# Retention values of a hybrid decoder layer by seven block products, with strided residue units between them

## The chip, the cores and the metric

One core of a Trainium2 chip runs the kernel. The metric is the device time of one execution in microseconds. Before the change it was 1881.49 us, the median of three runs (1881.42 to 1882.46). The work lies on these engines: PE (TensorE, matmuls; PEld its weight loads), DVE (VectorE), ACT (ScalarE), POOL (GpSimd, here also the accumulating DMAs) and SP (SyncE, which issues most DMAs).

## What is computed

Two decoder layers over 512 tokens of width 1024. Each projects the normed input once and mixes tokens in two ways in parallel. Cut to what matters here:

```python
def hybrid_layer(x, g_mix, w_in, ...):
    hn = rmsnorm(x, g_mix)
    proj = hn @ w_in
    qa, ka, va, qr, kr, vr, gr, ga, gb = split(proj)
    # A: dilated attention, 3 head groups with dilations 1, 4, 16 (va: 3 x 512 columns)
    # B: retention, 4 heads of 256 value columns (vr: 1024 columns)
    ...
    x = x + (sigmoid(ga) * y_a + sigmoid(gb) * y_b) @ w_o
    x = x + square(relu(rmsnorm(x) @ w_up)) @ w_down
```

The change is in how `va` (for the dilated groups) and `vr` are made, the value stage at the head of each layer.

## The kernel before

The program writes one instruction list for each engine by hand; engines meet through semaphores only. So the order in each list is the order of work. A layer consists of a value stage, four pairs of heads (queries, keys, attention, retention), gates, the output projection and the MLP. Weights are in single precision. To multiply them, ScalarE rounds each unit of weights (128 x 2048) to `w_hi` in two halves (`hi_halves`, L704 on), VectorE subtracts for `w_lo` (`lo_half`, L1175 on), and TensorE multiplies three terms (hi x hi, hi x lo, lo x hi). There are two buffers of `w_hi` and `w_lo`, and one of raw weights, `raw`, which SyncE fills half by half as VectorE is done with it (`lo_done`). The same split is made of the normed input: `h_hi`, `h_lo`, eight tiles of 128 x 512 (channels by tokens), counted by `h_ready`.

The value stage (`values_half`, L1925) has five groups g of 512 value columns, each of two units: g 0 for the attention group of dilation 1, g 1 and 2 for the retention's values, g 3 and 4 for the two attention groups that are ordered by residue (token modulo 4). A group has four banks of PSUM for the four token blocks and takes 96 matmuls of 512 columns. The banks of g 0 and g 1 differ (`vbanks`), and a group waits (`v_out`) for the evictions of the one two before it. For g 3 and 4, ScalarE copies `h_hi` and `h_lo` in residue order into `res_hi` and `res_lo` (`by_residues`, L745). The evictions scale with the token's inverse RMS. Retention values are split into hi and lo there (`vR_high`, L804, and VectorE's L1301), sent to DRAM by `vR_away` (L546), and brought back head by head by `vR_back` as `vR_hi`, `vR_lo` and `vR_last`.

After group 0, TensorE makes the mean of squares (`mean`), ScalarE its root (`rms`, L752 on), VectorE the reciprocal and the diagonal matrices. `spread` (L1840) has TensorE broadcast the inverse over the partitions, and `rms_spread` (L1223 on) has VectorE copy that to `rstd_all`; both stand at the end of the stage. SyncE's order in the stage is: weights of g 0 and 1, the inverse's residues by way of DRAM, weights of g 2, retention values away, weights of g 3, values away, weights of g 4, the spill of x to DRAM (`x_out`, L535), tables.

The MLP's down projection already multiplies by seven products of half blocks, with sums of operands by VectorE and sums of weights by accumulating DMAs from GpSimd (`sum_of`, `add_quarter`, slots `gh`).

## Time and profile before

| | |
|---|---|
| median of three runs | 1881.49 us |
| the profiled execution, all of it | 1880.63 us |
| its span from first to last instruction | 1878.8 us |
| mean granted TensorE clock | 0.999 |
| matmuls | 9064 |
| DMA moved | 236.93 MB, 126 GB/s in the mean |
| queue q1 (hardware) / q0 (software, accumulating) | 33.8% / 10.6% of 16 engines |

The page tells for each engine its busy time and share. Matmuls overlap in the records, since a recorded one (0.39 us) is longer than the distance of two starts; the starts give the rate. The waits show who kept an engine idle, and the timeline what lies beside what. In the first layer the value stage is 6.7 to 121.1 us, in the second 937.9 to about 1051 us.

### The profile page before, as it was taken

To read this page: it belongs to the slowest core of one execution; us is meant where nothing else is said; L and a number is where in the kernel's file an instruction comes from. 1 tells how busy PE (TensorE), PEld (TensorE's weight loads), DVE (VectorE), ACT (ScalarE), POOL (GpSimd) and SP (SyncE) were. 2 spreads that over 40 slices of the span, in tenths; PEclk is the share of its full clock that TensorE was granted. 3 is DMA by queue.
4 is the path that set the end of the run, shared out by engine and by line. 5 is a ranking of instruction groups with operands and counts; after the bars stand their busy time and mean duration, and the time that the engine had idled before them with its cause. 6 is when DMAs were issued, how large, how long until landed. Compare 5 with 4: busy or idle time off the path is not lost.

```text
span 1878.8 us, 22972 instructions
## 1 busy us (share of the span) xinstructions
PE 1863.8 (99%) x9064; PEld 1548.6 (82%) x9064; DVE 1255.0 (67%) x1848; ACT 837.6 (45%) x1234; POOL 129.0 (7%) x104
## 2 busy tenths in 40 slices
PE   9999999999999999999999999999999999999998
PEld 8888888887888888888788888888878888888886
DVE  5356778767447576776863568788674575667777
ACT  7325465464224344434472254554642233434445
POOL 0001111100000000000000112112000000000010
PEclk9999999999999999999999999999999999999999
DMA  4544233333333465557626333243243334655675
GB/s 147 202 157 121 82 90 113 89 98 90 129 97 123 124 145 133 139 139 202 150 86 241 95 109 104 74 121 105 68 145 99 105 113 112 135 149 142 135 210 126
DMA packets 210668, 236.93 MB, mean 126 GB/s; under 512 B 13569, under 2 KB 160769, under 8 KB 209537
## 3 DMA queue, kind: packets, MB, share of 16 engines
q1 hardware_dynamic: 192944, 201.03, 33.8%
q0 software_dynamic: 16896, 33.56, 10.6%
q8 instruction: 72, 1.18, 0.3%
q10 hardware_dynamic: 720, 0.87, 0.1%
q14 instruction: 36, 0.29, 0.1%
HBM read 219.57 MB, written 13.77 MB: 124 GB/s over the span
## 4 chain that ended last, share of the span: by engine, by line
PE 91%; DVE 4%; ACT 2%; DMA 2%; issue 1%; POOL 0%; DVEq 0%; ACTq 0%; POOLq 0%
PE pj L1853 20%; PE pj L1855 20%; PE pj L1854 20%; PE sc L2159 2%; PE sc L2161 2%; PE yr L2161 2%; PE yr L2159 2%; PE sc L2163 2%; PE yr L2163 2%; PE pt L2159 1%; DMA w_raw<-in_w_down 1%; PE pt L2161 1%; PE pt L2163 1%; DVE w_lo L1178 1%; PE yr L1960 1%; PE pt L1961 1%
## 5 line engine op out<-in xcount | busy, mean ns | idle before, releaser
L1853 PE MATMUL pj<-h_hi,w_hi 128*128 128x512 f32 x1408 | 554.4, 394 | 1.0 <-DVE sA L1553 1.0
L1855 PE MATMUL pj<-h_hi,w_lo 128*128 128x512 f32 x1408 | 548.5, 390 | 0.0
L1854 PE MATMUL pj<-h_lo,w_hi 128*128 128x512 f32 x1408 | 548.3, 389 | 0.0
L1178 DVE TENSOR_TENSOR w_lo<-w_raw,w_hi 128x1024 fp32r<-128x1024 f32 x283 | 334.9, 1220 | 129.0 <-ACT w_hi L707 127.8
L707 ACT CAST w_hi<-w_raw 128x1024 fp32r<-128x1024 f32 x280 | 282.9, 1050 | 291.8 <-PE pj L1855 56.9
L1853 PEld LDWEIGHTS pj<-h_hi,w_hi 128*128 128x128 f32 x1408 | 264.3, 188 | 59.1 <-issue 1.9
L1855 PEld LDWEIGHTS pj<-h_hi,w_lo 128*128 128x128 f32 x1408 | 264.2, 188 | 56.0
L1854 PEld LDWEIGHTS pj<-h_lo,w_hi 128*128 128x128 f32 x1408 | 264.4, 188 | 53.8 <-issue 0.5
L1132 POOL TENSOR_TENSOR rcos<-rot,tables 128x512 f32<-128x512 f32 x64 | 87.2, 1363 | 693.7 <-ACT rot L833 634.7
L1000 ACT ACTIVATE relu<-pj 128x512 f32<-128x512 f32 x64 | 38.2, 597 | 185.2 <-PE pj L1855 185.2
L722 ACT CAST w_hi<-gh 128x1024 fp32r<-128x1024 f32 x80 | 79.9, 1050 | 82.0 <-PE yr L2163 30.5
L1619 DVE TENSOR_TENSOR u<-relu,rstd_all 128x512 f32<-128x512 f32 x64 | 44.1, 690 | 100.9 <-ACT relu L1000 100.9
L1140 POOL DMA_DIRECT2D gh<-in_w_down x26 | 33.4, 1285 | 941.2 <-DVE w_lo L1178 911.2
L1178 DVE TENSOR_TENSOR w_lo<-gh,w_hi 128x1024 fp32r<-128x1024 f32 x80 | 94.2, 1219 | 1.8 <-ACT w_hi L722 1.8
L833 ACT COPY rot<-pj 128x512 f32<-128x512 f32 x48 | 27.9, 581 | 110.6 <-PE pj L1855 64.5
L1326 DVE TENSOR_TENSOR swp<-swp,tables 128x512 f32<-128x512 f32 x64 | 66.6, 1040 | 4.4 <-ACT swp L837 2.7
L2159 PE MATMUL sc<-w_hi,a_hi 128*128 128x512 f32 x160 | 62.6, 391 | 3.7 <-DVE w_lo L1178 3.2
L2159 PE MATMUL yr<-w_hi,a_hi 128*128 128x512 f32 x160 | 62.5, 391 | 0.0
L2161 PE MATMUL sc<-w_lo,a_hi 128*128 128x512 f32 x160 | 62.3, 389 | 0.0
L2163 PE MATMUL yr<-w_hi,a_lo 128*128 128x512 f32 x160 | 62.3, 389 | 0.0
L2163 PE MATMUL sc<-w_hi,a_lo 128*128 128x512 f32 x160 | 62.3, 389 | 0.0
L2161 PE MATMUL yr<-w_lo,a_hi 128*128 128x512 f32 x160 | 62.2, 389 | 0.0
(340 smaller groups left out, 3134.9 us busy)
## 6 DMA issues: line engine op xcount, KB each, us to landing
w_raw<-in_w_in SPq DMA_DIRECT2D x151, 512.0 KB, 4.7
w_raw<-in_w_up SPq DMA_DIRECT2D x64, 512.0 KB, 4.7
gh<-in_w_down POOLq DMA_DIRECT2D x26, 1024.0 KB, 8.7
gh<-in_w_down SPq DMA_DIRECT2D x16, 1024.0 KB, 5.8
w_raw<-in_w_down SPq DMA_DIRECT2D x20, 512.0 KB, 5.0
w_raw<-in_w_b SPq DMA_DIRECT2D x16, 512.0 KB, 3.5
w_raw<-in_w_o SPq DMA_DIRECT2D x16, 512.0 KB, 3.9
u<-in_w_down POOLq DMA_DIRECT2D x6, 1024.0 KB, 13.2
```

Of the source, the lines that this page charges most:

```text
L707: nc.scalar.copy(w_hi[s][:, c], raw[:, c]).then_inc(hi_done, 1)
L722: nc.scalar.copy(w_hi[n % 2][:, h], gh[slot][:, h]).then_inc(hi_done, 1)
L1132: nc.gpsimd.tensor_tensor(rcos[:], rot[:], cosA if u < 3 else cosR, ALU.mult).then_inc(rot_cos, 1)
L1178: nc.vector.tensor_tensor(w_lo[s][:, c], src[:, c], w_hi[s][:, c], ALU.subtract).then_inc(lo_done, 1)
L1326: nc.vector.tensor_tensor(swp[:], swp[:], sinA if u < GROUPS else sinR, ALU.mult).then_inc(rot_sin, 1)
L1619: nc.vector.tensor_tensor(to, relu[:, o, :], rstd_all[:], ALU.mult).then_inc(relu_scaled, 1)
L1853: nc.tensor.matmul(out, w_hi[s][:, wc], acts[0], start=first, stop=False)
L1854: nc.tensor.matmul(out, w_hi[s][:, wc], acts[1], start=False, stop=False)
L1855: return nc.tensor.matmul(out, w_lo[s][:, wc], acts[0], start=False, stop=last)
L2159: nc.tensor.matmul(out, hi[:, k, t], w_hi[s][:, w], start=opens and k == 0, stop=False, skip_group_check=not opens)
L2161: nc.tensor.matmul(out, hi[:, k, t], w_lo[s][:, w], start=False, stop=False, skip_group_check=not opens)
L2163: return nc.tensor.matmul(out, lo[:, k, t], w_hi[s][:, w], start=False, stop=k == 3, skip_group_check=not opens)
```

## The change

The retention's value product, (512 tokens x 1024 channels) by (1024 x 1024), is cut in halves on each side and made by seven products P1 to P7 of 256 tokens x 512 channels x 512 columns instead of eight, in the way of the down projection. VectorE makes four sums of blocks of the normed input; these are kept in `h32`, in single precision, where the residue copies were. Weight sums come by accumulating DMAs into the slots `gh`. Partial results share PSUM banks, and ScalarE (`value_read`) and VectorE (`value_finish`) bring them into `vP`, which lies where x lay, so that x must have been spilled. The two residue groups' four units R0 to R3 stand between the products, and their stationary operand is a strided view of `h_hi` and `h_lo`; `by_residues` is gone. Retention values go to DRAM and back in single precision, and each pair splits them again (`value_split`, on ScalarE and VectorE). The mean and spread stay, but `spread` stands ahead of R0 and `x_out` ahead of R0's weights. The queries' start waits for the residue evictions (`v_res`).

```diff
+    V_SEQ = [("G", 0), ("G", 1), ("P", 1), ("R", 0), ("P", 5), ("R", 1), ("P", 6), ("P", 3), ("R", 2), ("P", 7),
+             ("R", 3), ("P", 2), ("P", 4)]
 # SyncE
-                value_weights(0)
-                value_weights(1)
+                value_weights()
+                if l > 0:
+                    sp.wait_ge(lo_done, m_unit(l - 1, "D", CH - 1, 3) * 2 + 2 + UNIT_CREDIT)
+                value_slot(0)
+                value_slot(1)
+                x_out()
+                value_raw("R", 0)
                 residues_of_rstd()
-                value_weights(2)
-                vR_away(0)
-                value_weights(3)
-                vR_away(1)
-                value_weights(4)
-                x_out()
+                value_raw("R", 1)
+                value_raw("R", 2)
+                value_raw("R", 3)
+                vR_away(0, 1, 0)
+                value_raw("P", 2)
+                vR_away(1, 1, 2)
 # GpSimd
+                for i in (5, 6, 4, 7):
+                    add_values(i)
 # ScalarE
+                for s in range(1, VN):
+                    kind, i = V_SEQ[s]
+                    if s == 2:
+                        rms(l)
+                    if V_SEQ[s - 1] in (("P", 1), ("P", 5), ("P", 6)):
+                        value_read(V_SEQ[s - 1][1])
+                    value_high(s + 1)
+                    if (kind, i) in (("P", 1), ("R", 0), ("P", 5), ("P", 6)):
+                        set_high({("P", 1): 5, ("R", 0): 6, ("P", 5): 3, ("P", 6): 7}[kind, i])
+                value_read(4)
 # VectorE
+                for s in range(1, VN):
+                    kind, i = V_SEQ[s]
+                    if s == 2:
+                        rms(l)
+                        rms_diag(l)
+                        nc.vector.tensor_scalar(nrstd[:], rstd[:, 0:TB], -1.0, None, ALU.mult).then_inc(nrstd_done, 1)
+                    if V_SEQ[s - 1] in (("P", 3), ("P", 7), ("P", 2)):
+                        value_finish(V_SEQ[s - 1][1])
+                    if V_SEQ[s - 1] in (("R", 1), ("R", 3)):
+                        residue_values(V_SEQ[s - 1][1] // 2)
+                    value_low(s + 1)
+                    if s == 1:
+                        value_sum(5)
+                    if (kind, i) == ("P", 1):
+                        set_low(5)
+                        rms_spread(l)
+                        first_values()
+                        value_sum(6)
+                    if (kind, i) == ("R", 0):
+                        set_low(6)
+                        value_sum(3)
...
+                def value_split(J):
+                    dve.wait_ge(vr_hi, J + 1)
+                    nc.vector.tensor_tensor(vR_lo[:], vR[:, 0:TB - 1, :], vR_hi[:], ALU.subtract).then_inc(vr_lo, 1)
 # TensorE
+                def residues_half(u):
+                    n = v_unit(l, "R", u)
+                    for kk in range(4):
+                        k = 4 * (u % 2) + kk
+                        if kk % 2 == 0:
+                            weights(n, kk // 2)
+                        w = slice(kk * S, (kk + 1) * S)
+                        for b in range(TB):
+                            if k == 0 and u > 0:
+                                pe.wait_ge(v_res, l * 2 * TB + b + 1)
+                            elif k == 0 and b == 0:
+                                pe.wait_ge(v_out, l * VO + TB)
+                            elif k == 0 and b == 2:
+                                pe.wait_ge(std_done, l + 1)
+                            elif k == 0 and b == 3:
+                                pe.wait_ge(rstd_all_done, 2 * l + 1)
+                            hh, hl = (by_residue(v[:, k, :])[:, b] for v in h)
+                            nc.tensor.matmul(rbank[b], hh, w_hi[n % 2][:, w], start=(k == 0), stop=False)
+                            nc.tensor.matmul(rbank[b], hh, w_lo[n % 2][:, w], start=False, stop=False)
+                            mm = nc.tensor.matmul(rbank[b], hl, w_hi[n % 2][:, w], start=False, stop=(k == KT - 1))
+                    mm.then_inc(mm_done, 2)
+
+                values_half(0)
+                values_half(1)
                 mean(2 * l)
-                for g in range(1, VG):
-                    values_half(g, 0)
-                    values_half(g, 1)
-                pe.wait_ge(v_out, (l * VG + VG) * TB)
-                spread(l)
+                for kind, i in V_SEQ[V_U:]:
+                    if (kind, i) == ("R", 0):
+                        spread(l)
+                    if kind == "P":
+                        value_product(i)
+                    else:
+                        residues_half(i)
+                pe.wait_ge(v_res, (l + 1) * 2 * TB)
```

## Rows read from the trace of the kernel before

**Rows 1.** The page, part 1: busy us, share of the span, instructions.
```profile
PE 1863.8 (99%) x9064; PEld 1548.6 (82%) x9064; DVE 1255.0 (67%) x1848; ACT 837.6 (45%) x1234; POOL 129.0 (7%) x104
```

**Rows 2.** Waits of TensorE: total us, times, longest us.
```profile
PE sc L2159 <- DVE w_lo L1178: 3.2, 2, 1.6
...
PE yr L1960 <- ACT std L754: 0.3, 1, 0.3
```

**Rows 3.** Timeline, TensorE: start us, us, engine, line; 512 and 256 columns.
```profile
100.11 0.39 PE L1961 MATMUL pt<-w_lo,res_hi 128*128 128x512 f32 x1
100.11 0.19 PEld L1962 LDWEIGHTS pt<-w_hi,res_lo 128*128 128x128 f32 x1
100.33 0.39 PE L1962 MATMUL pt<-w_hi,res_lo 128*128 128x512 f32 x1
...
197.13 0.28 PE L2067 MATMUL yr<-ST_hi,vR_hi 128*128 128x256 f32 x1
197.25 0.28 PE L2068 MATMUL yr<-ST_lo,vR_hi 128*128 128x256 f32 x1
```

**Rows 4.** Timeline of the first layer: last h tile, start of group 1, the spread.
```profile
27.55 0.69 DVE L1203 TENSOR_TENSOR h_lo<-hn,h_hi 128x512 fp32r<-128x512 f32 x1 [0.69 <-ACT h_hi L743]
...
32.54 0.49 PE L1960 MATMUL yr<-w_hi,h_hi 128*128 128x512 f32 x1
...
120.28 1.05 PE L1844 MATMUL yr<-diag,ones 128*128 128x128 f32 x8
121.09 0.48 PE L1853 MATMUL pj<-h_hi,w_hi 128*128 128x512 f32 x1
```

**Rows 5.** Timeline of the second layer: last h tile, start of group 1.
```profile
955.97 0.68 DVE L1203 TENSOR_TENSOR h_lo<-hn,h_hi 128x512 fp32r<-128x512 f32 x1
...
963.06 0.49 PE L1960 MATMUL sc<-w_hi,h_hi 128*128 128x512 f32 x1
```

**Rows 6.** Issues; landings of the spill, of tables (min/median/max) and of weights.
```profile
91.73 0.47 SPq L538 DMA_DIRECT2D x_scratch<-x  x1
92.24 0.43 SPq L574 DMA_DIRECT2D tables<-in_tables  x1
...
x_scratch<-x SPq DMA_DIRECT2D x2, 2048.0 KB, 10.0
...
DMA to landing us min/median/max: 11.9/12.8/13.6
...
w_raw<-in_w_in SPq DMA_DIRECT2D x151, 512.0 KB, 4.7
```

**Rows 7.** Groups by line and shape: count, busy us, mean ns, idle before.
```profile
L707 ACT CAST w_hi<-w_raw 128x1024 fp32r<-128x1024 f32 x280 | 282.9, 1050 | 291.8 <-PE pj L1855 56.9 <-DMA w_raw<-in_w_down 49.9 <-DMA w_raw<-in_w_in 47.2
L1178 DVE TENSOR_TENSOR w_lo<-w_raw,w_hi 128x1024 fp32r<-128x1024 f32 x283 | 334.9, 1220 | 129.0 <-ACT w_hi L707 127.8 <-ACT w_hi L766 1.2
36.13 1.40 DVE L1292 TENSOR_SCALAR vA<-sc,rstd 128x512 f32<-128x512 f32 x2
```

**Rows 8.** Accumulating DMAs: count, size, median us from issue to landing.
```profile
gh<-in_w_down POOLq DMA_DIRECT2D x26, 1024.0 KB, 8.7
```

**Rows 9.** Groups by line and shape: copies and sums, strided and contiguous.
```profile
L748 ACT CAST res_hi<-h_hi 128x512 fp32r<-128x512 f32 x16 | 17.7, 1108 | 0.0
L743 ACT CAST h_hi<-hn 128x512 fp32r<-128x512 f32 x23 | 14.0, 610 | 4.1 <-DVE hn L1190 4.1
L1333 DVE TENSOR_TENSOR qk<-rcos,swp 128x512 f32<-128x512 f32 x32 | 34.4, 1075 | 1.1
L1331 DVE TENSOR_TENSOR qk<-rcos,swp 128x512 f32<-128x512 f32 x16 | 11.1, 692 | 0.5
```

**Rows 10.** Timeline of the first pair: last exponential, the transposes that wait.
```profile
190.31 0.19 ACT L845 ACTIVATION_READ_ACCUMULATOR x<-x,stats 128x1 f32 x1
...
194.15 1.04 PE L2015 MATMUL sc<-ident,prob 128*128 128x128 f32 x8
```

**Rows 11.** Weight loads of the warm-up matmuls: ns min/median/max, first and last start.
```profile
L1803 PEld LDWEIGHTS yr<-ones x20: 192/333/338, 1.0 to 5.9; 128*128 128x128 f32 x20
```

More of the change, by code:

```diff
@@ L380, in trunk @@
         st_lo = sem("st_lo")
+        v_in = [sem(f"v_in{i}") for i in range(2)]
+        v_added = [sem(f"v_added{i}") for i in range(2)]
+        v_res = sem("v_res")
+        v_first = sem("v_first")
+        v_sum = sem("v_sum")
+        v_set_hi = sem("v_set_hi")
+        v_set = sem("v_set")
+        nrstd_done = sem("nrstd_done")
+        vr_sent = [sem(f"vr_sent{i}") for i in range(4)]
+        vr_in = sem("vr_in")
         vr_hi = sem("vr_hi")
-        vr_sent = sem("vr_sent")
-        vr_in = sem("vr_in")
+        vr_lo = sem("vr_lo")
         ret_mm = sem("ret_mm")
@@ L852, in probT_out @@
                     if j == 2:
-                        act.wait_ge(x_spilled, l * 16 + 16)
+                        for part in range(4):
+                            act.wait_ge(vr_sent[part], (l + 1) * 32)
                         act.wait_ge(y_done, J + 1)
@@ L868, in key_high @@
                     act.wait_ge(rot_out, J * 8 + 6 + o + 1 + 1)
-                    act.wait_ge(x_spilled, l * 16 + 16)
+                    for part in range(4):
+                        act.wait_ge(vr_sent[part], (l + 1) * 32)
                     nc.scalar.copy(qkR_hi[:, o, :], qkR[:, o, :]).then_inc(key_hi, 1)
+                def value_split(J):
+                    act.wait_ge(vr_in, J * 16 + 16)
+                    nc.scalar.copy(vR_hi[:], vR[:, 0:TB - 1, :]).then_inc(vr_hi, 1)
                 def st_high(J, j):
@@ L1100, in added_tile @@
                         act.wait_ge(hn_done, (2 * l + 2) * KT + j + 1)
-                        nc.scalar.copy(h_hi[:, k, :], hn[:, j % 2, :]).then_inc(h_hi_done, 1)
+                        nc.scalar.copy(h_hi[:, k, :], h32[:, k, :]).then_inc(h_hi_done, 1)
                         if j >= 2:
@@ L1344, in masked @@
                     elif j == 1:
-                        dve.wait_ge(x_spilled, l * 16 + 16)
+                        for part in range(4):
+                            dve.wait_ge(vr_sent[part], (l + 1) * 32)
                     nc.vector.memset(tick[:, j % 2:j % 2 + 1], 0.0)
@@ L1843, in spread @@
                 for b in range(TB):
-                    mm = nc.tensor.matmul(spread_bank[l][:, b * P:(b + 1) * P], ones[:], diag[:, b, :], start=True, stop=True)
+                    mm = nc.tensor.matmul(spread_bank[:, b * P:(b + 1) * P], ones[:], diag[:, b, :], start=True, stop=True)
                 mm.then_inc(spread_done, 1)
@@ L1963, in values_half @@
+                            hh, hl = h_hi[:, k, b * P:(b + 1) * P], h_lo[:, k, b * P:(b + 1) * P]
+                            nc.tensor.matmul(out, hh, w_hi[n % 2][:, w], start=(j == 0), stop=False)
+                            nc.tensor.matmul(out, hh, w_lo[n % 2][:, w], start=False, stop=False)
+                            mm = nc.tensor.matmul(out, hl, w_hi[n % 2][:, w], start=False, stop=(j == KT - 1))
                             if j == KT - 1 and b < TB - 1:
                                 mm.then_inc(v_done, 1)
-                        if l > 0 and g == 0 and j == 0:
+                        if l > 0 and j == 0:
@@ new lines, in value_product @@
+                def value_product(i):
+                    n = v_unit(l, "P", i)
+                    value_ready(i)
+                    opens = i in (1, 5, 2)
+                    for k in range(4):
+                        if k % 2 == 0:
+                            weights(n, k // 2)
+                        w = slice(k * S, (k + 1) * S)
+                        for b in range(2):
+                            if i in (1, 2, 4):
+                                hi, lo = (value_operand(i, v, k, b) for v in h)
+                            else:
+                                hi, lo = (v[:, k, b * P:(b + 1) * P] for v in a_sets[(V_SUMS.index(i) + 1) % SETS])
+                            out = vbank(l, i)[:, b * S:(b + 1) * S]
+                            nc.tensor.matmul(out, hi, w_hi[n % 2][:, w], start=opens and k == 0, stop=False,
+                                             skip_group_check=not opens)
+                            nc.tensor.matmul(out, hi, w_lo[n % 2][:, w], start=False, stop=False,
+                                             skip_group_check=not opens)
+                            mm = nc.tensor.matmul(out, lo, w_hi[n % 2][:, w], start=False, stop=k == 3,
+                                                  skip_group_check=not opens)
+                    mm.then_inc(mm_done, 2)
@@ L2070, in ret @@
                         else:
-                            mm = nc.tensor.matmul(out, vR_last[:, v], ST_last[:], start=False, stop=True)
+                            mm = nc.tensor.matmul(out, vR[:, TB - 1, v], ST_last[:], start=False, stop=True)
                     mm.then_inc(ret_mm, 1)
```

335 lines of the change are left out of this document (190 added, 145 removed).

## The prediction, made before the change was run

> **What bounds the kernel now.** The page first: TensorE is busy 99% of a span of 1878.8 us, VectorE 67%, ScalarE 45% [rows 1]. A busy matmul can still hide waits, so I read the waits of TensorE next: the longest sum is 3.2 us, in two waits [rows 2]. The order of the matmuls sets the time; every other engine runs in its shadow. Then the timeline of the value stage, for the price of one matmul: with 512 columns streamed they start at 100.11 and 100.33, 0.227 us unrounded (512 columns a matmul; 384 of them lie between 32.54 and 120.28 [rows 4], 0.2285 us each with the one wait among them), and each weight load of 0.19 us starts with the matmul before it [rows 3]. So a removed matmul of 512 columns gives 0.227 us, if nothing new stops the engine.
>
> The profiled execution took 1880.63 us (span 1878.8 plus 1.83 around it); the median of the runs is 1881.49, 0.86 us more. I sum against the first and add the 0.86 at the end.
>
> **Matmuls removed.** Per layer, before: five groups of 96 matmuls, 480. After: group 0 as it is (96), seven products of 4 x 2 x 3 = 24 (168), four residue units of 4 x 4 x 3 = 48 (192), together 456. That is 24 fewer a layer, 48 in all: 48 x 0.227 = -10.9 us. The standard deviation's wait of 0.3 us (ACT std) [rows 2] goes too, since ScalarE no longer copies residues ahead of it: -0.3 us.
>
> **Work of the other engines.** Sixteen pairs of residue copies (eight a layer) at 1.11 us each [rows 9] leave ScalarE, and seven products bring 14 casts of 1.05 and 14 subtractions of 1.22 us a layer [rows 7] in place of 8 and 8, four sums and eight splits of 1.05 to 1.22 us. In a product of 24 matmuls (5.44 us) VectorE has some 2.44 for the next weights, 1.22 for a sum, 1.22 for a split: 4.9 us, just inside. After a residue unit it evicts four banks (2.8) ahead of the next weights: 2.8 + 2.4 = 5.2 of 5.44 us, of which only the first half of the weights is needed at once. I cost all this at nothing; without that cover each of some four such joints would cost under 1 us. The accumulating DMAs take 8.7 us from issue to landing [rows 8], and between the users of a slot lies at least a residue unit of 48 x 0.227 = 10.9 us plus a product; the tightest is product 7's, cast about 11 us or more after its add may start. Nothing again, with up to 2 us as the other end. In the attention stage each pair gains a ScalarE cast and a VectorE subtraction of 128 x 768, bounded by the 1.05 and 1.22 us of 1024 elements. They stand ahead of the last mask; the last exponential ended at 190.5 and the transposes that wait for it began at 194.15 [rows 10], so 3.6 us cover it: nothing. If that cover failed, up to 1 us a pair, 8 us.
>
> **Where a new wait arises: the start of the first residue unit, R0.** Three pieces of code meet. (1) TensorE's first matmul of R0 waits for `v_out` of all four evictions of group 0, because R0 writes into the same PSUM banks. Before, group 1 had banks of its own. (2) VectorE makes these evictions behind the low part of R0's weights, the split of operand 5, and `rms_spread`; and the spread's matmuls stand on TensorE behind product 1. (3) SyncE issues the 2 MB spill of x (`x_out`) just ahead of R0's weights. Before, it stood at the end of the stage, with the tables alone right behind it [rows 6].
>
> Layer 0, step by step. The last h tile is there at 27.55 + 0.69 = 28.2, so the spill goes out at 28.3. In the trace the spill landed 10.0 us after its issue, and 1 MB issued 0.5 us behind it took 11.9 and 13.6 us, so 12.4 to 14.1 from the spill's issue [rows 6]; half a megabyte by itself takes 4.7 [rows 6]. R0's weights are such a megabyte: middle 13.2, 41.5. The accumulating DMA for product 5 (VectorE done with product 1's weights at about 33) now runs beside it on the same DMA engines; it adds between 0 and 6 us, I take 2, by its 8.7 us being shared with the queue: 43.5. Then in series: cast 1.05, low part 1.22, split of operand 5 1.22, the copy to rstd_all 0.69 as for VectorE's other 512 columns [rows 9], four evictions at 0.70 apart 2.8 [rows 7]: 7.0, so R0 can start at 50.5. TensorE is there much earlier: the first matmul behind the mean stood at 32.54 [rows 4], plus 24 x 0.227 = 5.44, plus the spread's 0.81 (120.28 to 121.09; it is only moved) [rows 4]: 38.8. Idle: 11.7 us. Layer 1: last h tile 955.97 + 0.68 = 956.65 [rows 5], plus 13.2 + 2 + 7.0 = 978.8; TensorE is ready at 963.06 [rows 5] + 6.25 = 969.3. Idle: 9.5 us. Together +21.2 us. Low end: if the weights were early, only spread, rstd_all and evictions would be left behind product 1: 0.69 + 2.8 + hops of 0.2 = 3.7 a layer, 7.4. High end: 14.1 and a contention of 6 us: 4.9 more a layer, 31.
>
> **TensorE's clock.** The mean granted clock is 0.999, so the higher level all along, but the first loads of `ones`, after idleness, took 333 ns in the median and 192 at the least [rows 11], about the ratio of 1.2 to 2.4 GHz; the transposes and loads between 1.0 and about 5.5 us were slow alike. Work done at the lower level for 4.5 us loses half of it, 2.2 us. A stall of ten microseconds occurs nowhere in this trace, so whether it brings the lower level is open: 0 to 2.2 each. I take 2.2, since the start is the nearest row: +4.4 us. After a stall of 3.7 us I take nothing.
>
> **The strided stationary operand.** 384 matmuls (192 a layer) load their weights with a step of four elements. The load has cover: with the same loads of 128 columns, matmuls of 256 columns start 0.12 us apart [rows 3], so a load occupies its path for at most 0.12 us and up to 0.11 us of a 0.227 us pitch is free. ScalarE's copy of 128 x 512 takes 1.11 us strided and 0.61 us contiguous, VectorE's sum 1.08 against 0.69 [rows 9]. By ScalarE's difference, 0.97 ns an element, 128 elements cost 0.124 us: 0.015 us over the cover, or 384 x 0.015 = +6 us. By VectorE's 0.75 ns, 0.096 us: hidden, 0. Far end: the whole load of 0.188 us stretched by 1.8 with nothing overlapping, +0.15 us x 384 = +58 us; below nothing is excluded, as no load gets shorter. I take 0, because a matmul hides the larger part in any case and VectorE's row fits in the cover.
> A page of the Trainium skill, "Advanced Engine Details and Errata", section SBUF Cachelines, speaks against this edit: at least two hits on a 16-byte line are needed, and a step of four single-precision elements gives one. It names no figure; by this rule the sum would get the 6 us, by the cover alone none.
>
> **Sum.** -10.9 - 0.3 + 21.2 + 4.4 + 0 = +14.4. 1880.63 + 14.4 = 1895.0, and 0.86 more gives 1895.9 us against the median. I forecast 1895.5.
>
> **Rivals.**
> A, the forecast: R0's weights come behind the spill and VectorE's series follows. 0.50; its own range is 1886 to 1903 by the contention (0 to 6) and the clock (0 to 4.4).
> B, the same, with loads beyond their cover: +6, 1902. For it, ScalarE's row; against, VectorE's. 0.20.
> C, the other side: the spill doesn't hold R0's weights back. Place: SyncE's queue between x_out and R0. It decides at the point where R0's second half has landed by 36 us in layer 0 (its cast, low part and the split of operand 5 then end with the spread). Then 7.4 us of stall are left: 1881.5 - 11.2 + 7.4 = 1877.7, just on the edge of faster. For it: weights land 4.7 us after their issue in the median [rows 6]. Against: [rows 6], where the follower landed after the spill in both layers. 0.16, half of it beyond 0.2%.
> D, the evictions are done by the time product 1 ends, and all of the gain comes: 1870.3. Against: the spread's place in TensorE's order. 0.04.
> E, loads far over their cover, or joints later in the stage that fail (product 3 behind the four evictions, product 7 behind its add): 1907 to 1960. 0.10. That the change doesn't do what it says, with as many matmuls as before, the count of the loops excludes.
>
> **Range and chances.** A and B hold 0.70, half of C 0.08, a strip of E 0.03: 1878 to 1906. A measurement tells about 0.2%, 3.8 us, from no change. Faster beyond that (under 1877.7): half of C and D, 0.11. Within it: the other half of C and A's lower edge, 0.11. Slower: 0.78.
>
> **What would show it.** After the change the two stretches of the value stage should show TensorE idle ahead of the first `pt<-h_hi` matmul of R0, 12 and 10 us, released by VectorE's vA, and the cast of R0's weights waiting for its DMA, issued after x_scratch, with a landing of 12 us or more. The matmul count falls by 48. The pitch in R0 to R3 is 0.227 us (0.24 for B). The stretches from group 0's end to the first queries take 88.55 + 6 to 8 us. Wrong would be a landing under 8 us (C), or idle time at other places.

## The result and the profile after

The changed kernel takes 1896.76 us in the median (1895.02 to 1899.99 in four runs), the kernel before 1881.57 us (1881.42 to 1882.46) beside it: a ratio of 1.008, 95% interval 1.0067 to 1.0093. It is slower by 15 us, inside the range and 1.3 us from the forecast. Five later runs of the same kernel on another chip gave 1890.76 us (1889.97 to 1895.94), ratio 1.0051 (1.0037 to 1.0065): slower too, by 9 us. Where those 6 us between the two series come from is one of the questions below.

The profiled execution spans 1896.5 us, 17.7 more than before. First the page's busy line, against [rows 1], and the first and longest waits of TensorE, against [rows 2] (total us, times, longest us):

```profile
PE 1861.3 (98%) x9016; PEld 1560.7 (82%) x9016; DVE 1289.9 (68%) x1882; ACT 832.7 (44%) x1234; POOL 140.4 (7%) x112
...
PE pt L2139 <- DVE vA L1393: 19.8, 2, 12.8
PE sc L2334 <- DVE w_lo L1251: 3.2, 2, 1.6
```

48 matmuls fewer, as counted, and busy time of TensorE 2.5 us less (not 10.9: the busy time of the slow and the strided matmuls has grown). One line is new, the rest of the list is that of before, without the wait for the standard deviation: 19.8 us in two waits, both the first matmul of R0, both ended by VectorE's vA. That is the place that the forecast named.

Layer 0 in the timeline, answering to [rows 4] (start us, duration us, engine, line, what, idle before and its releaser):

```profile
28.33 0.34 SPq L577 DMA_DIRECT2D x_scratch<-x  x1
...
28.71 1.42 SPq L514 DMA_DIRECT2D w_raw<-in_w_in  x2
...
32.59 0.49 PE L2114 MATMUL yr<-w_hi,h_hi 128*128 128x512 f32 x1
...
38.18 1.05 PE L1969 MATMUL pj<-diag,ones 128*128 128x128 f32 x8
...
39.23 1.04 ACT L755 CAST w_hi<-w_raw 128x1024 fp32r<-128x1024 f32 x1 [0.73 <-DMA w_raw<-in_w_in]
...
40.31 1.23 DVE L1251 TENSOR_TENSOR w_lo<-w_raw,w_hi 128x1024 fp32r<-128x1024 f32 x1 [0.55 <-ACT w_hi L755]
...
41.45 1.22 DVE L1374 TENSOR_TENSOR a_lo<-sq,a_hi 128x1024 fp32r<-128x1024 f32 x1
...
42.58 0.69 DVE L1298 COPY rstd_all<-pj 128x512 f32<-128x512 f32 x1
...
43.30 1.41 DVE L1393 TENSOR_SCALAR vA<-sc,rstd 128x512 f32<-128x512 f32 x2
...
44.63 1.40 DVE L1393 TENSOR_SCALAR vA<-pt,rstd 128x512 f32<-128x512 f32 x2
...
46.18 0.78 PE L2139 MATMUL pt<-w_hi,h_hi 128*128 128x512 f32 x1 [6.95 <-DVE vA L1393]
...
126.35 0.39 PE L1978 MATMUL pj<-h_hi,w_hi 128*128 128x512 f32 x1
```

Read it upwards from the stalled matmul: four evictions, the copy to rstd_all, the split of operand 5, the low part and the cast, which waited for its DMA, which stands in SyncE's queue behind the spill. From the landing (39.2) to R0 (46.18) it takes 6.95 us. The stage from product 1 to the first queries lasts 126.35 - 32.59 = 93.76 us where it was 88.55 [rows 4].

Layer 1, answering to [rows 5]:

```profile
963.01 0.34 SPq L577 DMA_DIRECT2D x_scratch<-x  x1
...
963.40 1.42 SPq L514 DMA_DIRECT2D w_raw<-in_w_in  x2
...
969.42 0.49 PE L2114 MATMUL sc<-w_hi,h_hi 128*128 128x512 f32 x1
...
975.26 1.04 ACT L755 CAST w_hi<-w_raw 128x1024 fp32r<-128x1024 f32 x1 [5.40 <-DMA w_raw<-in_w_in]
...
981.94 1.04 ACT L755 CAST w_hi<-w_raw 128x1024 fp32r<-128x1024 f32 x1 [5.64 <-DMA w_raw<-in_w_in]
...
982.41 0.34 SPq L572 DMA_DIRECT2D rstd<-rstd_scratch  x1
...
1068.77 0.39 PE L1978 MATMUL pj<-h_hi,w_hi 128*128 128x512 f32 x1
```

The same chain, but the second half of R0's weights landed 18.0 us after its issue, at 981.9. Hardly 0.5 us later SyncE could read the reciprocals back: their write of 512 elements of 4 bytes (L569), issued at 970.1, had just landed as well. The stage lasts 99.35 us (before: 1051.06 - 963.06 = 88.00). The landings of R0's two halves, minimum, median and maximum, in layer 0 and in layer 1:

```profile
DMA to landing us min/median/max: 8.7/9.3/10.0
...
DMA to landing us min/median/max: 11.8/14.9/18.0
```

Last the clock, from a table by stretch (from and to, length, busy us and instructions of PE, PEld, DVE, ACT and POOL, granted clock, DMA share, GB/s): the stall of layer 0, what follows it, and the rest of the stage. The DMA share is not used here; in a short stretch it can come out above 1.

```profile
38.20:46.18 7.98, 1.03 (x10) 0.87 (x8) 7.07 (x9) 3.46 (x5) 0.00 (x0) 0.89 1.32 99
46.18:51.20 5.02, 5.02 (x12) 4.04 (x13) 1.12 (x2) 1.21 (x2) 0.00 (x0) 0.50 0.82 172
51.20:125.00 73.80, 73.80 (x321) 68.31 (x320) 38.86 (x40) 24.05 (x26) 3.85 (x3) 1.00 0.54 136
```

For 5 us after the stall TensorE ran at 0.50, that is 1.2 of 2.4 GHz: 11 or 12 matmuls at a pitch of 0.43 us in place of 0.235.

### The profile page after: what moved, and what is told of

It is laid out like the page before. It is cut to its first block, busy times and chain, and to the rows that moved or that the text cites. A ratio compares the mean times of both kernels' runs of the same rounds, so it can differ in the third digit from the quotient of the medians.

```text
span 1896.5 us, 22965 instructions
## 1 busy us (share of the span) xinstructions
PE 1861.3 (98%) x9016; PEld 1560.7 (82%) x9016; DVE 1289.9 (68%) x1882; ACT 832.7 (44%) x1234; POOL 140.4 (7%) x112
## 4 chain that ended last, share of the span: by engine, by line
PE 89%; DVE 5%; DMA 3%; ACT 2%; issue 1%; SPq 0%; POOL 0%; DVEq 0%; ACTq 0%; POOLq 0%
PE pj L1978 20%; PE pj L1980 20%; PE pj L1979 20%; DMA w_raw<-in_w_in 2%; PE sc L2334 2%; PE sc L2336 2%; PE sc L2338 2%; PE yr L2338 2%; PE yr L2334 2%; PE yr L2336 2%; PE pt L2334 1%; PE pt L2336 1%; DMA w_raw<-in_w_down 1%; PE pt L2338 1%; DVE w_lo L1251 1%; PE pt L2139 1%
## 5 line engine op out<-in xcount | busy, mean ns | idle before, releaser
L1251 DVE TENSOR_TENSOR w_lo<-w_raw,w_hi 128x1024 fp32r<-128x1024 f32 x271 | 321.0, 1221 | 111.9 <-ACT w_hi L755 110.6
L755 ACT CAST w_hi<-w_raw 128x1024 fp32r<-128x1024 f32 x268 | 270.9, 1049 | 269.6 <-DMA w_raw<-in_w_in 62.9
L1251 DVE TENSOR_TENSOR w_lo<-gh,w_hi 128x1024 fp32r<-128x1024 f32 x104 | 122.5, 1220 | 16.2 <-ACT w_hi L853 13.8
```

Source lines behind the costliest of these rows:

```text
L755: nc.scalar.copy(w_hi[s][:, c], raw[:, c]).then_inc(hi_done, 1)
L1251: nc.vector.tensor_tensor(w_lo[s][:, c], src[:, c], w_hi[s][:, c], ALU.subtract).then_inc(lo_done, 1)
```

## The experiments

Theory: R0 starts late because (a) its weights come behind the spill of x, (b) VectorE makes the evictions behind the low part of those weights, and (c) the lower clock follows the stall. Rivals: that the loss is the strided operand, or a stage short of bandwidth, in which a stall taken away here comes up elsewhere.

**R0's weights ahead of the spill.**

```diff
-                x_out()
                 value_raw("R", 0)
+                x_out()
```

> The changed kernel with one thing different: SyncE issues R0's weights ahead of the spill of x. My theory (the landing behind the spill, then VectorE's series): R0's weights are in place during product 1, only spread, rstd_all and the four evictions are left behind product 1, 3.7 us a layer, in place of 7.0 and 12.8. Idle time falls by 12.4 us, and TensorE has no long stretch at 1.2 GHz behind it (2.4 and 2.2 us less): 1896.8 - 17 = 1880. Rival, contention: the spill now runs beside product 5's accumulating DMA, whose landing (16.6 us in layer 0) holds product 5 instead: 2 to 5 us come back, 1882 to 1885. Rival, the evictions' place alone decides: under 3 us gained, 1894 or more.

Measured: 1885.7 us (1883.74 to 1889.04), ratio 1.0021 (1.0012 to 1.0031). The waits of TensorE:

```profile
PE pt L2139 <- DVE vA L1393: 7.3, 2, 3.6
```

And the start of R0 in layer 0, from its timeline (the second row three matmuls after the first):

```profile
45.01 0.79 PE L2139 MATMUL pt<-w_hi,h_hi 128*128 128x512 f32 x1 [3.63 <-DVE vA L1393]
...
46.45 0.63 PE L2139 MATMUL pt<-w_hi,h_hi 128*128 128x512 f32 x1
```

3.63 us here and 3.64 us in layer 1, the floor of 3.7 a layer that the prediction worked out from the copy, the evictions and the hops. So the place of the spill is worth 19.8 - 7.3 = 12.5 us of waiting against the first profile of the changed kernel, and 7.0 against the control's below. But the clock falls after 3.6 us of idleness too (1.44 us for three matmuls): 7 matmuls in layer 0 and 14 in layer 1 were slow, 1.4 and 2.9 us.

**The evictions ahead of the low part of R0's weights**, the spill still first.

```diff
-                    value_low(s + 1)
+                    if s == 2:
+                        first_values()
+                        lo_half(n, n % 2, 0)
+                        rms_spread(l)
+                        lo_half(n, n % 2, 1)
+                        set_low(5)
+                        value_sum(6)
```

> The changed kernel with one thing different: VectorE evicts group 0 directly after the reciprocal, ahead of R0's weights, and copies rstd_all between the two halves of their low part. The spill stays ahead of R0's weights. My theory: R0 starts with the first half of the weights (layer 0: 39.8 in place of 46.2; layer 1: 977.6 in place of 988.9), but then stands again at its second half and at rstd_all; about 5 us less idle time in each layer, 1896.8 - 10 = 1887, and with the idle time in two pieces perhaps less time at the lower clock: 1884 to 1889. Rival, the weights' landing alone decides: 1893 or more. Rival, the evictions alone: 1880.

Measured: 1879.82 us (1876.42 to 1883.31), ratio 0.9986 (0.9977 to 0.9996), 7 us better than I had expected. R0 started at 39.85 and 971.70 with waits under 0.5 us, although the spill still went first: it had cost so much only because four evictions, a copy and a split stood behind it. A wait of 2.2 us at P5 in layer 0 is new, and eight matmuls behind it were slow. Against the changed kernel this edit is worth 11 to 17 us, the other one alone 5 to 11.

**Both edits.**

> Both edits together, R0's weights ahead of the spill and the early evictions. My theory: no idle time over 0.5 us is left ahead of R0 and no lower clock; what remains of the change is 48 matmuls fewer (-10.9), the wait for the deviation (-0.3) and the strided loads' 0.2345 against 0.2267 us (+3.0): 1881.6 - 8.2 = 1873.4, faster than before. Rival, contention: product 5's weights come late in layer 0, since the add lands 16.6 us after its issue at 33.3, and 2 to 4 us come back: 1875 to 1878. Rival, the seven products cost time by themselves somewhere else: 1880 or more.

Measured: 1881.08 us (1879.92 to 1882.8), ratio 0.9989 (0.998 to 0.9998): no better than the second alone, 8 us short of my sum. R0 no longer waits at all; P5 does, in layer 0:

```profile
52.94 1.99 ACT L853 CAST w_hi<-gh 128x1024 fp32r<-128x1024 f32 x2 [13.15 <-DMA gh<-in_w_in]
...
55.38 0.76 PE L2118 MATMUL sc<-w_hi,a_hi 128*128 128x512 f32 x1 [4.46 <-DVE w_lo L1251]
```

The stretch behind that wait, in the table by stretch (columns as above):

```profile
55.38:58.80 3.42, 3.42 (x8) 2.72 (x9) 3.42 (x4) 2.51 (x4) 1.29 (x1) 0.52 0.06 4
```

ScalarE waited 13.15 us for the accumulating DMA of P5, which landed 19.4 us after its issue, against 8.7 in the median [rows 8]. That the spill is the cause is not shown by this; the last group of experiments on the landings, below, speaks for another transfer. In the changed kernel the stall at R0 had hidden the late landing. The second view is the clock again: 0.52 for 3.4 us after a wait of 4.5. Together they are 6 of the 8 us. This is the rival of moved waiting, in part.

**The stall filled with matmuls that nobody reads** (28 in layer 0, 54 in layer 1, on `h_hi` and `ones`).

```diff
                     if (kind, i) == ("R", 0):
                         spread(l)
+                        pe.wait_ge(std_done, l + 1)
+                        for _ in range((28, 54)[l]):
+                            nc.tensor.matmul(pj[1][:], ones[:].bitcast(F32R), h_hi[:, 0, :], start=True, stop=True)
```

> The changed kernel with 28 (layer 0) and 54 (layer 1) matmuls of 512 columns more, whose result nobody reads, between the spread and R0. They fill about 6.3 and 12.2 us of TensorE's idle time. Nothing else is changed, and R0 can't start earlier by them. My theory of the clock: after the idle time TensorE runs at 1.2 GHz, 0.43 us a matmul, for 5.0 and 4.4 us; with the engine busy it stays at 2.4 GHz and R0's first matmuls stand 0.235 us apart: 2.2 and 2.0 us less, 1896.8 - 4.4 = 1892.4. Rival, the slow first matmuls of R0 come from the strided loads or from the DMA traffic: no change, 1896.8, or a little over where the added matmuls overrun the wait.

Measured: 1892.1 us (1891.15 to 1893.78), ratio 1.0048 (1.0031 to 1.0065), the number expected. The first matmuls of R0 in layer 0:

```profile
48.48 0.60 PE L2139 MATMUL pt<-w_hi,h_hi 128*128 128x512 f32 x1 [0.66 <-DVE vA L1393]
48.92 0.40 PE L2140 MATMUL pt<-w_lo,h_hi 128*128 128x512 f32 x1
49.16 0.40 PE L2141 MATMUL pt<-w_hi,h_lo 128*128 128x512 f32 x1
```

In layer 0 R0 starts 13.65 us behind the first product's start, as late as before (13.59), and then runs at full pitch. So the slow matmuls come from the idle time, and neither from the strided loads nor from the DMA traffic. Their price in the run time is not shown by this experiment, and the match with 1892.4 is luck. In layer 1 of the profiled execution R0's two halves landed early (minimum, median, maximum):

```profile
DMA to landing us min/median/max: 8.7/9.2/9.7
```

VectorE's evictions ended at 979.1 us, but the 54 added matmuls held TensorE until 986.84, 7.7 us longer. The expectation said only that R0 can't start earlier by them; it can start later.

**Contiguous slices in place of every fourth token**, in the changed kernel (the residue values are then those of other tokens).

```diff
-                            hh, hl = (by_residue(v[:, k, :])[:, b] for v in h)
+                            hh, hl = (v[:, k, b * P:(b + 1) * P] for v in h)
```

> The changed kernel with contiguous 128-token blocks as stationary operand of the residue units, no other edit; it leaves out the residue ordering of the tokens, so the values are those of other tokens. Theory: the stall of 19.8 us stays as it is and only the 8.6 ns for each of the residue matmuls at full clock go, about 360 of them: 3 us, 1893.7 us, ratio to the kernel before 1.0065. Rival, the stride costs nothing and the sum was off elsewhere: 1896.8 us, ratio 1.008.

Measured: 1890.03 us (1889.4 to 1895.51), ratio 1.0051 (1.0038 to 1.0065). This is twice the gain that I expected, but it can't be put down to the stride: its six times fall into two groups, four around 1889.6 and two around 1895, and the wait ahead of R0 in layer 1 was 7.8 us in its profile, not 12.8, with a landing after 13.0 us. Something that the edit does not touch scatters.

**The changed kernel once more**, as a control.

> The changed kernel once more, unedited, as a control for the wait ahead of R0 in layer 1: 12.8 us in its first profile, 10.4 in the version with the late accumulating DMA, 7.8 in the one with contiguous slices, whose times fell into two groups (1889.5 and 1895). If the landing of R0's second half scatters by itself from execution to execution, this profile may show any wait from 7 to 13 us in layer 1 and the times spread over 1890 to 1900; if the stride or the edits set it, the wait is 12 to 13 us again and the times lie at 1895 to 1898. Layer 0's wait should be 7 us either way.

Measured: 1890.76 us (1889.97 to 1895.94): four times from 1890.0 to 1892.2, one of 1895.9. The waits in the profile are 7.1 and 7.3 us, R0's second half in layer 1 landed after 12.5 us. So the wait in layer 1 scatters in the very kernel that is studied, by 5.5 us. The value stage of layer 1 lasts 93.2 us here and 99.35 in the first profile, which accounts for the 6.1 us between the spans of the two profiled executions. That the executions without a profile divide in the same way is likely and not shown.

**What makes that landing scatter?** Two transfers run beside R0's weights: the accumulating DMA for P5, and the write of the reciprocals. Three kernels move one, the other, and both. First the accumulating DMA, held until R0's casts are done:

```diff
+                    if i == 5:
+                        pool.wait_ge(hi_done, v_unit(l, "R", 0) * 2 + 2)
```

> The changed kernel, where the accumulating DMA for P5 (1 MB, GpSimd's queue) waits until R0's weights are cast, so that it no longer runs beside them and the spill. Theory, it is this transfer that made the landings of R0's halves 8.7 and 10.0 us in layer 0 and up to 18.0 us in layer 1: the landings come near 8 us in both; the wait at R0 falls from 6.95 to about 5.5 us and from 12.8 to about 5.5 us, and P5, which is wanted 10.9 us after R0 starts, may wait 0 to 2 us for its late DMA: 1896.8 - 8.7 - 1.5 for the clock + 1 = 1888 to 1891 us, ratio to the kernel before 1.004. Rival, the landings are long because of the spill of 2 MB ahead of them: landings and waits as in the changed kernel, 1896 to 1898 us.

Measured: 1896.25 us (1895.31 to 1898.17), ratio 1.0075 (1.0063 to 1.0087). R0's second half landed after 10.1 us in layer 0, as before, and after 15.6 in layer 1. No gain: this theory of mine fell. Then only the round trip of the reciprocals, moved behind R1's weights:

```diff
-                residues_of_rstd()
                 value_raw("R", 1)
+                residues_of_rstd()
```

> The changed kernel, where the round trip of the reciprocals through DRAM (512 elements of 4 bytes each way) is issued behind R1's weights and not 6 to 7 us behind R0's. Theory: in layer 1 the second half of R0's weights landed at 981.9 us, just as that round trip's write did, while the bulk of the traffic had gone at 978.4 us; the tiny packets hold up the tail of R0's weights on the same queue. Then its landing falls from 18 to 9 or 10 us, the wait at R0 in layer 1 from 12.8 to 6 or 7 us as in layer 0, and the time to 1889 to 1891 us, ratio to the kernel before 1.0045. Rival: the spill of 2 MB and the weights alone are behind the late landing; then waits of 7 and 10 to 13 us, 1895 to 1898 us. R1 may win or lose up to 1 us, since its weights no longer wait for the round trip.

Measured: 1893.16 us (1891.01 to 1894.62), ratio 1.0058 (1.0045 to 1.007). The wait in layer 1 is 7.9 us, the second half's landing 13.1 us, and none of the five times lies in the upper group, but the median is above that of the control beside it (1890.76): by itself not conclusive. So I repeated the first and ran both together:

> The same edit as in e6 once more (the accumulating DMA for P5 waits for R0's casts; the write of the reciprocals stays 6 to 7 us behind R0's weights). In e6 R0's second half landed at 979.7 us in layer 1, 0.7 us ahead of that write's landing at 980.4, and all five times lay from 1895.3 to 1898.2. If R0's second half comes late by being caught with the write of the reciprocals, this happens again: a landing of 14 to 18 us, a wait of 10 to 13 us in layer 1, 1894 to 1898 us. If it is scatter that no transfer beside it sets, any value from 7 to 13 us may come, and times from 1889 to 1898.

Measured: 1896.62 us (1894.99 to 1897.9), ratio 1.0075 (1.0062 to 1.0087).

> The changed kernel with neither of the two transfers beside R0's weights: the accumulating DMA waits for R0's casts, and the round trip of the reciprocals is issued behind R1's weights. The spill of 2 MB ahead of R0's weights stays. Theory, what comes beside R0's weights makes the late and scattered landing in layer 1: both layers' landings are 9 to 10 us and steady, both waits 6 to 7 us, all times within 1888 to 1891 us, ratio 1.004. Rival, the spill alone does it: the landing in layer 1 scatters from 11 to 18 us as before, the wait there is 7 to 13 us, times from 1890 to 1898 us.

Measured: 1890.78 us (1889.46 to 1891.83), ratio 1.0042 (1.0028 to 1.0055). The landings of R0's halves in layer 1, min/median/max, of the repeated kernel:

```profile
DMA to landing us min/median/max: 9.0/12.0/14.9
```

and in its timeline the casts that wait for them and the read-back of the reciprocals, which waits for their write:

```profile
972.95 1.05 ACT L755 CAST w_hi<-w_raw 128x1024 fp32r<-128x1024 f32 x1 [2.65 <-DMA w_raw<-in_w_in]
...
979.28 1.04 ACT L755 CAST w_hi<-w_raw 128x1024 fp32r<-128x1024 f32 x1 [5.28 <-DMA w_raw<-in_w_in]
...
979.91 0.34 SPq L572 DMA_DIRECT2D rstd<-rstd_scratch  x1
```

The same two views of the kernel with neither:

```profile
DMA to landing us min/median/max: 9.8/10.2/10.6
```

```profile
972.68 1.05 ACT L755 CAST w_hi<-w_raw 128x1024 fp32r<-128x1024 f32 x1 [3.36 <-DMA w_raw<-in_w_in]
...
973.91 1.05 ACT L755 CAST w_hi<-w_raw 128x1024 fp32r<-128x1024 f32 x1 [0.18 <-DMA w_raw<-in_w_in]
```

With the reciprocals' write beside them, R0's second half lands 5.9 us behind the first and 0.6 us ahead of that write. In the other execution with this edit it was 5.7 us behind the first and 0.7 ahead of the write, in the first profile of the changed kernel 6.7 behind and 0.5 ahead. With neither transfer beside them the halves land 0.8 us apart, and all five times lie within 2.4 us.

That looks like a cause, but the rest of the traces does not bear it out. The landings of R0's second half in layer 1, over the nine profiled executions in which its weights stand behind the spill:

| the write of the reciprocals beside them | landing, us from issue |
|---|---|
| yes, accumulating DMA too | 18.0, 13.0, 12.5, 12.0, 9.7 |
| yes, accumulating DMA held back | 15.6, 14.9 |
| no, accumulating DMA beside them | 13.1 |
| no, neither | 10.6 |

The 9.7 is that of the kernel with the added matmuls, which had both transfers in place and landed earlier than the kernel with neither. Where the landing came early, the write landed 6 to 10 us later than it. In layer 0 the second half landed after 9.9 to 10.1 us in all nine, whatever ran beside it. What can be said: the three latest landings all came 0.5 to 0.7 us ahead of the write's, and in one of them the DMA engines moved nothing (0 GB/s) from 974 to 979 us while the landing at 979.3 was still waited for, so there it was not a lack of bandwidth. Two executions without the write are too few to say that its absence prevents this, and what decides stays open.

Nor do the times decide it. All ten of the kernel with the held-back DMA lie from 1895 to 1898, but in its two profiled executions only 3.8 and 2.8 us of the excess over the control's lie in the value stage of layer 1 (96.9 and 96.0 us against 93.2). Another 2.3 and 2.6 us lie behind it, where the down projection of layer 1 waited two or three times for VectorE's low part and in the control once. So there is a second place that scatters. And the kernel with neither has the control's median, 1890.8; against the kernel before beside it the ratios are 1.0042 and 1.0051, with intervals that overlap.

The same traces say more about what makes the accumulating DMA for P5 late: the write of the reciprocals, and not the spill alone. With the write of the reciprocals issued 0.9 us behind it in layer 0 and 3.9 us in layer 1, it landed after 16.6 to 19.4 us in layer 0 and 13.4 to 17.0 in layer 1, in all seven profiled executions of that kind. With the write behind R1's weights, spill and R0's weights still beside it, it took 11.1 and 13.8 us. In the kernel with neither beside R0, the held-back DMA was issued after the spill had landed, with the write again 1.0 and 1.1 us behind it: 14.2 and 16.6 us. In the kernel with both edits, the write in flight, the DMA engines moved 15 to 45 GB/s from 36 to 45 us; the write landed at 44.1, and from 47 us on they moved 225 and more. In the version below, with the write issued later, they moved 174 to 311 GB/s from 36 to 45 us. The edit that moves the write also issues R1's weights earlier, and why 512 elements of 4 bytes should hold up a megabyte is not shown.

**The version made from these results**: both edits of above, R1 put ahead of P5 (so that the accumulating DMA has one more residue unit), and R1's weights ahead of the round trip of the reciprocals.

```diff
-    V_SEQ = [("G", 0), ("G", 1), ("P", 1), ("R", 0), ("P", 5), ("R", 1), ("P", 6), ("P", 3), ("R", 2), ("P", 7),
-             ("R", 3), ("P", 2), ("P", 4)]
+    V_SEQ = [("G", 0), ("G", 1), ("P", 1), ("R", 0), ("R", 1), ("P", 5), ("R", 2), ("P", 6), ("P", 3), ("R", 3),
+             ("P", 7), ("P", 2), ("P", 4)]
...
-                residues_of_rstd()
                 value_raw("R", 1)
+                residues_of_rstd()
```

> The version with both reorderings (R0's weights ahead of the spill of x; the layer's first values scaled right behind the reciprocal) had no wait at R0 but 4.5 us at P5 in layer 0, behind an accumulating DMA that took 19.4 us beside the spill, and 3.4 us at the lower clock after it. Here R1 is put ahead of P5, so that this DMA has a residue unit of 10.9 us more, and R1's weights are loaded ahead of the round trip of the reciprocals (which in that version held them back to 44.5 us). Own theory, the transfers are only late and not too many: no wait at P5 and full clock, minus 4.5 and minus 1.7 us; R1's weights are issued at 39.2 and 41.4 us, land 9.4 us later, are cast and split at 51 and 53 us against a start of R1 at 50.2 us, so up to 1 us of wait in each layer is new. Span 1879.2 - 6.2 + 1 = 1874 us, time 1873 to 1877, ratio to the kernel before 0.996. Rival, the stage lacks bandwidth and the wait only moves: 4 us or more at R1 or R2, time 1879 to 1882. A third outcome would be a new wait of the residue values for the reciprocals, whose round trip now starts behind R1's weights at 42 us, takes up to 18 us and is wanted at 61 us.

Measured: 1878.67 us (1876.71 to 1880.21), ratio 0.9979 (0.9971 to 0.9988): the lowest median of the kernels here that leave nothing out, though its interval overlaps that of the evictions' edit alone (0.9977 to 0.9996); 3 us ahead of the kernel before and 12 to 18 ahead of the changed one. Its profile spans 1874.8 us; no wait at R0, R1, P5 or any other unit of the value stage is left, and the granted clock is 1.00 in it. New are waits of 1.6 and 1.2 us of the first queries for their weights, one in each layer, behind two products in a row. The accumulating DMA for P5 landed 8.7 us after its issue in layer 0, at 42.0, and not after 19.4: with the write of the reciprocals out of its way a landing at 42.0 would have been in time for the old order too, so that R1's new place may not have been needed. No run tests the two edits one by one. The median is 2 us above the range that I expected, and I did not look further into that.

**The same with contiguous slices** (values of other tokens), to price the stride with no stall beside it.

> The kernel of e8_seq with one more edit: in the residue units the stationary operand is the contiguous 128-token block and not every fourth token, so that the residue values are computed for the wrong tokens, with the same number and shapes of matmuls. It measures the price of the stride with no stall beside it. Theory: weight loads of 308 ns fall to 188 ns and the pitch of the residue units from 0.235 to 0.227 us, 8.6 ns times 376 of 384 matmuls, 3.2 us less than e8_seq (a ratio 0.0017 lower). Rival, the pitch in the trace is a matter of how ends are modelled and the stride is free: within 1 us of e8_seq. Second rival, a load of 308 ns exceeds a pitch of 227 ns and only half of it is hidden, 80 ns times 376: 30 us, which the pitch of 0.235 speaks against.

Measured: 1875.78 us (1872.94 to 1877.12), ratio 0.9963 (0.9951 to 0.9975), 2.9 us below its neighbour in the same series. Two matmuls of R0 in the timeline of the strided version, 18 starts apart, and under them its loads by line (ns min/median/max); then the same of the contiguous version, 17 starts apart:

```profile
41.02 0.40 PE L2144 MATMUL pj<-w_lo,h_hi 128*128 128x512 f32 x1
...
45.26 0.40 PE L2144 MATMUL pt<-w_lo,h_hi 128*128 128x512 f32 x1
```

```profile
L2143 PEld LDWEIGHTS pt<-w_hi,h_hi x64: 308/309/310, 39.1 to 1026.5; 128*128 128x128 f32 x64
```

```profile
41.08 0.39 PE L2144 MATMUL pj<-w_lo,h_hi 128*128 128x512 f32 x1
...
44.94 0.39 PE L2143 MATMUL pt<-w_hi,h_hi 128*128 128x512 f32 x1
```

```profile
L2143 PEld LDWEIGHTS pt<-w_hi,h_hi x64: 186/188/192, 39.4 to 1025.4; 128*128 128x128 f32 x64
```

4.24 / 18 = 0.2356 us against 3.86 / 17 = 0.2271: 8.5 ns a matmul, 3.3 us for 384 of them, and 2.9 in the medians (whose spreads, 3.5 and 4.2 us, make this a support more than a proof). The queries of the contiguous version waited 4.1 us for their weights where those of its neighbour waited 2.8, which takes back a part of the gain.

## Why the prediction was right

The number was right, most steps too, and some errors cancelled. In the order of the sum:

- **Matmuls, -10.9 us.** The count fell by 48 and the pitch of the products is 0.227 us. Right. The wait for the standard deviation (-0.3) is gone.
- **The mechanism of the stall.** Place, releaser and order of the series were right: `pt<-h_hi` of R0, ended by vA, the cast behind its DMA behind the spill. The series of 7.0 us measured 6.95. The floor of 3.7 us a layer with early weights, worked out for rival C, measured 3.63 and 3.64 once R0's weights went first.
- **Its size in layer 0, 11.7 us: wrong by 4.7.** The mis-sized term is the landing. I took 15.2 us from the spill's issue, from tables that landed behind a spill of 10.0 us [rows 6]; here the spill landed in 7.5 us, the second half 39.2 - 28.3 = 10.9 us after the spill's issue. The allowance of 2 us for the accumulating DMA has no counterpart: with that DMA held back the landings in layer 0 were the same (8.5 and 10.0 us from their issues).
- **Its size in layer 1, 9.5 us:** measured 12.8, and 7.3 in the control. The landing was 18.9 us behind the spill's issue, 3.7 later than my 15.2, and 13.4 in the control. I gave one landing for what turned out to be a spread: over the nine executions the second half took 9.7 to 18.0 us. I listed what is queued ahead of R0's weights and beside them on GpSimd's queue, and not what follows them on SyncE's, the write of the reciprocals. The three latest landings ended just ahead of that write's; whether it causes them stays open.
- **The sum of both, 21.2 us, measured 19.8** (14.3 in the control). One layer was taken 4.7 us too long and the other 3.3 too short, and the forecast hit the slower outcome. Against the control it would have been 5 us too high. That the total came within 1.3 us is luck; the sign and the place are not.
- **The clock, +4.4 us.** From the pitches, 2.3 us in layer 0 and 2.1 in layer 1: 4.4. The nearest row [rows 11] gave the right size. Wrong was the statement beside it, that a stall of 3.7 us costs nothing in clock: after 3.6 us the slow matmuls cost 1.4 and 2.9 us. In rival C's sum these 4 us are missing: its 1877.7 would have been 1885, with the stride, and the kernel that makes it true measured 1885.7. So C, had it come true, would have been slower than the kernel before, and the half of its chance that I gave to "faster" belonged elsewhere.
- **The strided operand, 0 us (rival B +6).** Neither: the load grew from 188 to 308 ns, by 0.120 us, as ScalarE's difference had suggested (0.124), but the matmul hides all but 8.5 ns of it, 3.1 us for the 362 matmuls at full clock. B had the mechanism, and its price was twice too high.
- **Costs taken at nothing.** No wait in the rest of the value stage, none new in the attention stage: right for the changed kernel. The cover of the accumulating DMA was named as a residue unit and a product against 8.7 us and up to 2. The landing took 16.6 us in layer 0, about twice the 8.7 of [rows 8]; the cast of P5 waited 7.6 us for it, and only the stall at R0 kept this from TensorE, as the versions without the stall showed with 2.2 and 4.5 us.
- **What would show it.** 12 and 10 us of idleness: 7 and 13. A landing of 12 us or more: 10.0 in layer 0, 18.0 in layer 1. The stretches, 88.55 + 6 to 8: +5.2 and +11.4.

The account of the profile: -10.9 - 0.3 + 19.8 + 4.4 + 3.1 = +16.1 of 17.7 us. By the stretches 16.6 lie in the value stages and 1.1 outside them, spread over small waits that I can't assign.

The Trainium skill, "Advanced Engine Details and Errata", section SBUF Cachelines, wants at least two hits on a 16-byte line to absorb the access latency. The loads agree with it (308 against 188 ns, one hit against four). The page doesn't say how much of that a matmul covers; here it was all but 8.5 ns of 120.

The Trainium skill, "DMA: Bandwidth & Descriptors", section Queues, rings and completion order, says that a transfer's semaphore write is ordered behind every earlier write of the same DMA engine, across its queues. By this rule a completion can be held back by small writes of another transfer, which would fit the three landings 0.5 to 0.7 us ahead of the reciprocals' write; no run here shows that order itself, and the four executions in which the half landed 6 to 10 us ahead of the write leave it a conjecture.

## What to carry to other kernels

Before work is saved on the busiest engine, look at each joint that the change creates: what must be evicted first, what stands ahead of that on the evicting engine, and what stands ahead of its input in the DMA queue. Here 10.9 us of matmuls were saved, and 14 to 20 us of waiting and 4 of lower clock were bought by one buffer reused at once; scaling the old contents before the next weights are split, an edit of order alone, gave all of it back. When a stall goes, look at the transfer that it had hidden, and keep a write of 4-byte elements out of the stretch in which an accumulating DMA is on its way: moved back, it brought that landing in layer 0 from 16.6 to 11.1 us. And before two landings are explained by what runs beside them, collect the same landing from every trace that has it.

## What the hardware showed beyond that

- After a wait of only 3.6 us TensorE's matmuls started 0.43 us apart (1.2 GHz) for 3 to 6 us, for 3.4 us after a wait of 4.5, and for eight matmuls after one of 2.2 us (the evictions' edit, P5). After one of 2.8 us (first queries of the last kernel above) they did not slow. A filled stall left the clock at the higher level. After the waits of 3.6 us and more the slow stretch was 7 to 14 matmuls long, 1.4 to 2.9 us of loss, with no relation to the length of the wait in these runs.
- A single-precision weight load of 128 x 128 with a step of four elements took 308 ns against 188, and made the matmuls behind it start 8.5 ns further apart.
- An accumulating DMA of 1 MB landed after 13.4 to 19.4 us with a write of 512 elements of 4 bytes issued 1 to 4 us behind it, after 11.1 and 13.8 without that write beside the same spill and weights, against 8.7 in the median [rows 8]. The small write itself took 8.8 to 16.3 us to land.
- The time of one and the same kernel fell into two groups (1890 to 1892 and 1895 to 1900 us). In the one traced execution of each, the difference was one landing of 12.5 or 18.0 us in one layer. Without the repeated run the contiguous version would have been credited with 6.7 us where the stride costs 3.
